# Stick-breaking attention on one core: two heads per ScalarE and VectorE operation, the gate made transposed, the values product turned round

## The chip, the cores and the metric

One core of a Trainium2 chip runs the whole program. The metric is device time in microseconds (us) from launch to end, lower is better. TensorE (PE in the profile, its weight loads PEld) multiplies, ScalarE (ACT) applies functions, VectorE (DVE) does elementwise work, GpSimd (POOL) small side jobs, SyncE (SP) issues most DMAs.

## The reference

Three layers of a small network over 256 tokens of width 1024 are computed one after the other. The change lies in the second, the stick-breaking attention with 16 heads of 64:

```python
def stick_breaking_attention(q, k, v):          # (B, H, S, d)
    for blk in range(S // Q_BLOCK):             # Q_BLOCK = 128, S = 256
        logits = einsum('bhtd,bhsd->bhts', q[:, :, t0:L], k[:, :, :L]) * SB_SCALE
        mask = s_idx < t_idx
        log_keep = where(mask, log_sigmoid(-logits), 0.0)
        later = cumsum(log_keep, reverse=True) - log_keep
        a = where(mask, exp(log_sigmoid(logits) + later), 0.0)
        outs.append(einsum('bhts,bhsd->bhtd', a, v[:, :, :L]))

    # in the block around it
    k_all, v_all = split(rms_norm(x, kv_norm) @ w_kv, 2)
    k_sh, v_sh = rms_norm(heads(k_all), k_norm), heads(v_all)
    q, z = split(rms_norm(x, b_norm) @ b_w_in, 2)
    q = rms_norm(heads(q), b_q_norm)
    o = stick_breaking_attention(q, k_sh, v_sh)
    x = x + (o * silu(z)) @ b_w_out
```

## The kernel before, in words

Each engine runs a program written out by hand, and semaphores tie them together. TensorE multiplies in float32r with both operands split into a high and a low part, so one product of 128x128 by 128x512 is three matmuls (L735, L736, L737). The activations are turned into hT_hi and hT_lo (contraction in the partitions, 256 tokens in the columns); in `product` a piece of hT is stationary and 512 weight columns move.

**Weights.** A block of 1024 x 512 lands in a ring of two and is split in two halves: ScalarE writes whi, then VectorE wlo. The split buffers hold three halves, so the split of a half (`refill(name, half)`, three halves ahead) can begin once TensorE has used the named half. These splits, the copies of results out of PSUM and the head norms stand in a fixed order on ScalarE and VectorE. TensorE's order here is: products k, v, transposes of k ("T k"), product q, product zb (the gate z), with the transposes of q amid it. Each stage has two products of 512 columns (nb = 0, 1). The head norm of half of k or q is `half_means` on VectorE (squares, sum, mean), a power on GpSimd, `half_scale` on VectorE.

**The loop.** 16 heads go in 8 pairs, j = 0 to 7; each head has its bank of PSUM (six banks in turn). For pair j TensorE makes the logits transposed, keys in the partitions, 384 columns a head (`stick_logits`, L885 to L891). ScalarE makes log(1 + exp(-|x|)) of them by Abs (L1465), Exp (L1466), Ln (L1480); VectorE adds max(x, 0) to it (L2085) and splits the sum into sp_hi and sp_lo (L2090, L2094); TensorE then adds the cumulative sums into the same bank (`stick_logs`, L898, L901, L903), ScalarE takes the Exp (L1473, the weights a), and TensorE multiplies by the values (`stick_values`, L912 to L914). LAG is 2, and on TensorE iteration j holds logits(j), logs(j-2), values(j-3); on ScalarE it is Abs and Exp of the first head of j, the two L1473 of j-2, Abs and Exp of the second head, two Ln of j. logits(j) needs the banks of pair j-3, so it waits for both L1473 of j-3. Three `ple` products (L844) stand ahead of logs(0), a fourth after the loop.

**After the loop** the gated result h is turned on TensorE (`turn("o1", ...)`, L728), split by ScalarE (L1303) and VectorE (L1708), and goes into product b_out.

## Time and profile before

| what | value |
|---|---|
| time, median of 3 runs | 868.62 us (868.02 to 869.25) |
| span of the profiled execution, first to last instruction | 866.2 us |
| PE, PEld, DVE, ACT busy | 851.7, 737.0, 591.9, 441.4 us |
| loop, from logits(0) to the fourth ple | 213.13 to 248.33 us |

The profiled execution has only its span; a time of its own outside the span is not given. The span is 2.4 us below the median of the runs, which is what launch and end add. Busy times overlap between engines and, for matmuls, within TensorE: a matmul of 512 columns is listed with some 0.39 us though the next one starts 0.23 us after it. Distances between starts are therefore what counts on TensorE.

### The profile page before, as it was taken

The numbers are of one execution on the slowest core, as the hardware profiler recorded it, in microseconds if no ns is written. First come the engines' busy times: TensorE is split into PE (matmuls) and PEld (weight loads), VectorE is DVE, ScalarE is ACT, GpSimd is POOL, SyncE is SP. The second block draws the span as 40 slices with busy tenths as digits, with TensorE's granted clock in tenths as the row PEclk, the third lists the DMA queues.
The fourth block names the chain that finished last, engine by engine and source line by source line (L and its number), as shares of the span: only waits on it lengthen the run. The fifth ranks groups of instructions, "written<-read, shape, count | busy, mean of one in ns | idle before, by whom it ended". The sixth has DMA issues, their size and how long they took to land.

```text
span 866.2 us, 13480 instructions
## 1 busy us (share of the span) xinstructions
PE 851.7 (98%) x5659; PEld 737.0 (85%) x5659; DVE 591.9 (68%) x738; ACT 441.4 (51%) x591; POOL 117.3 (14%) x74
## 2 busy tenths in 40 slices
PE   8999999999999999999999999999989999999998
PEld 7887888888788887888988889997868999999996
DVE  5684677666756678888788788786975655555553
ACT  6644466556953656754553446443164644444441
POOL 0100001111000004123144344540000000000000
PEclk9999999999999999999999999999999999999999
DMA  9927645555004436226455565556976465555621
GB/s 332 372 75 246 239 146 196 194 194 184 11 22 154 160 98 244 97 97 210 157 198 167 207 231 195 209 190 140 282 265 235 151 210 182 188 190 194 194 98 48
DMA packets 68405, 155.96 MB, mean 180 GB/s; under 512 B 3145, under 2 KB 6954, under 8 KB 68346
## 3 DMA queue, kind: packets, MB, share of 16 engines
q1 hardware_dynamic: 65312, 146.80, 50.1%
q0 software_dynamic: 2224, 7.67, 2.6%
q10 hardware_dynamic: 810, 0.63, 0.5%
q8 instruction: 45, 0.74, 0.3%
q14 instruction: 14, 0.11, 0.0%
HBM read 146.70 MB, written 7.34 MB: 178 GB/s over the span
## 4 chain that ended last, share of the span: by engine, by line
PE 91%; DVE 6%; ACT 2%; issue 1%; DMA 0%; ACTq 0%; DVEq 0%
PE bank L735 19%; PE bank L736 19%; PE bank L737 19%; PE bank L1062 7%; PE bank L1064 7%; PE bank L1060 7%; PE bank L728 3%; PE bank L844 2%; PE bank L834 1%; PE bank L946 1%; PE bank L885 1%; DVE pT L1826 1%; PE bank L1133 1%; PE bank L1122 1%; DMA vrows<-in_vecs 0%
## 5 line engine op out<-in xcount | busy, mean ns | idle before, releaser
L1725 DVE TENSOR_TENSOR wlo<-ring,whi 128x2048 fp32r<-128x2048 f32 (+1 forms) x103 | 251.7, 2449 | 135.3 <-ACT whi L1334 135.0
L1334 ACT ACTIVATE whi<-ring 128x2048 fp32r<-128x2048 f32 (+1 forms) x104 | 198.4, 1909 | 208.3 <-PE bank L737 143.2
L735 PE MATMUL bank<-whi,hT 128*128 128x512 f32 (+1 forms) x512 | 201.6, 394 | 3.2 <-DVE wlo L1955 1.4
L737 PE MATMUL bank<-whi,hT 128*128 128x512 f32 (+1 forms) x512 | 198.8, 388 | 0.0
L736 PE MATMUL bank<-wlo,hT 128*128 128x512 f32 (+1 forms) x512 | 198.7, 388 | 0.0
L1060 PE MATMUL bank<-hT,whi 128*128 128x256 f32 x512 | 145.3, 284 | 0.0
L1062 PE MATMUL bank<-hT,whi 128*128 128x256 f32 x512 | 144.9, 283 | 0.0
L1064 PE MATMUL bank<-hT,wlo 128*128 128x256 f32 x512 | 144.8, 283 | 0.0
L735 PEld LDWEIGHTS bank<-whi,hT 128*128 128x128 f32 x512 | 96.1, 188 | 25.0 <-issue 2.7
L737 PEld LDWEIGHTS bank<-whi,hT 128*128 128x128 f32 x512 | 96.1, 188 | 19.6
L736 PEld LDWEIGHTS bank<-wlo,hT 128*128 128x128 f32 x512 | 96.2, 188 | 19.0 <-issue 0.5
L1060 PEld LDWEIGHTS bank<-hT,whi 128*128 128x128 f32 x512 | 98.2, 192 | 0.6
L1062 PEld LDWEIGHTS bank<-hT,whi 128*128 128x128 f32 x512 | 98.2, 192 | 0.5
L1064 PEld LDWEIGHTS bank<-hT,wlo 128*128 128x128 f32 x512 | 98.2, 192 | 0.0
L735 PE MATMUL bank<-whi,hidT_hi 128*128 128x512 f32 x224 | 88.0, 393 | 0.0
L736 PE MATMUL bank<-wlo,hidT_hi 128*128 128x512 f32 x224 | 87.4, 390 | 0.0
L737 PE MATMUL bank<-whi,hidT_lo 128*128 128x512 f32 x224 | 87.2, 389 | 0.0
L1720 DVE SCALAR_TENSOR_TENSOR wlo<-ring,vcols,whi 128x512 fp32r<-128x512 f32 x64 | 43.8, 745 | 20.6 <-ACT whi L1330 20.6
L1330 ACT ACTIVATE whi<-ring,vcols 128x512 fp32r<-128x512 f32 x64 | 40.9, 711 | 19.3 <-PE bank L737 17.0
L735 PEld LDWEIGHTS bank<-whi,hidT_hi 128*128 128x128 f32 x224 | 42.1, 188 | 9.7 <-issue 1.2
L737 PEld LDWEIGHTS bank<-whi,hidT_lo 128*128 128x128 f32 x224 | 42.1, 188 | 9.0
L736 PEld LDWEIGHTS bank<-wlo,hidT_hi 128*128 128x128 f32 x224 | 42.1, 188 | 8.2
(296 smaller groups left out, 1026.9 us busy)
## 6 DMA issues: line engine op xcount, KB each, us to landing
ring<-in_w_ff SPq DMA_DIRECT2D x64, 1024.0 KB, 5.3
ring<-in_ple_gate_w SPq DMA_DIRECT2D x8, 1024.0 KB, 5.0
ring<-in_w_kv SPq DMA_DIRECT2D x8, 1024.0 KB, 5.0
ring<-in_b_w_in SPq DMA_DIRECT2D x8, 1024.0 KB, 5.0
ring<-in_a_w_in SPq DMA_DIRECT2D x7, 1024.0 KB, 13.1
ring<-in_w_in SPq DMA_DIRECT2D x6, 1024.0 KB, 5.8
ring<-in_w_glu SPq DMA_DIRECT2D x6, 1024.0 KB, 10.1
ring<-in_a_w_out SPq DMA_DIRECT2D x4, 1024.0 KB, 5.7
```

The lines of the kernel that those rows point to most:

```text
L728: last = pe.transpose(b[0:width, cc * S + t * P:cc * S + t * P + P], src[:, t, c * width:(c + 1) * width], ident)
L735: pe.matmul(bank_cols, high[:, at[0], at[1]], w_high, start=first, stop=False)
L736: pe.matmul(bank_cols, high[:, at[0], at[1]], w_low, start=False, stop=False)
L737: return pe.matmul(bank_cols, low[:, at[0], at[1]], w_high, start=False, stop=last)
L844: last = pe.matmul(b[:, :], pT[:, l, k, t * P:(t + 1) * P], ple_rows[:, k, nb * 512:(nb + 1) * 512], start=(k == 0), stop=(k == 1))
L1060: pe.matmul(b[:, at:at + S], w_high[:, kk, cols], hT_hi[:, k, :], start=k == 0 and at == 0, stop=False, skip_group_check=True)
L1062: pe.matmul(b[:, at:at + S], w_high[:, kk, cols], hT_lo[:, k, :], start=False, stop=False, skip_group_check=True)
L1064: last = pe.matmul(b[:, at:at + S], w_low[:, kk, cols], hT_hi[:, k, :], start=False, stop=k == KC - 1, skip_group_check=True)
L1330: ins = act.activation(whi[at][:, n], ring[:, slot[name], cols][:, n], ACT.Copy, scale=gain(gained[name[0]], 4 * (g % 2) + kk))
L1334: act.activation(whi[at], raw_rows(g), ACT.Copy).then_inc(high_made, 1)
L1720: ins = dve.scalar_tensor_tensor(out=wlo[at][:, n], in0=ring[:, slot[name], cols][:, n], scalar=gain(gained[name[0]], 4 * (g % 2) + kk), i ...
L1725: dve.tensor_tensor(wlo[at], raw_rows(g), whi[at], ALU.subtract).then_inc(low_made, 1)
```

## The change

1. **Loop.** The eight banks become one tensor, and `bank_pair` views the two banks of a pair as 2 x 384 columns. Abs, Exp, Exp of the logs, Ln and the three VectorE operations run once per pair on 768 columns. On ScalarE the order is now Abs(j), Exp(j), Exp of the logs(j-2), Ln(j).
2. **Values.** `stick_values` takes a pair: the 64 value columns of a head are stationary, the weights a move (256 and 128 columns). The even head writes partitions 0 to 63, the odd head 64 to 127, so the result is already transposed.
3. **Gate.** z is made transposed by `turned_product`: 128x128 pieces of the weights are stationary and 256 token columns of hT move. Since the norm's scale per token now lies along the columns, `rows_of_rstd` makes a row of it in all partitions: VectorE fills two diagonal tiles (`diag`), TensorE multiplies them by a matrix of -1, VectorE copies the result. VectorE multiplies z by it (`z_out`), and ScalarE takes Silu afterwards from SBUF.
4. **After the loop.** The transposes of o1 are gone; oz = o times gate is split into hT_hi and hT_lo by ScalarE (`oz_split`) and VectorE (`oz_low`), for the most part within the loop's last iterations.
5. **Order.** The products now stand as k, q (with the rows between its two halves), T k, zb (with T q amid it), v, loop; the weight loads likewise.

```diff
-    for stage in ("k", "v"):
-        for nb in range(2):
-            product(stage, nb, (stage, nb), turned_by="kv" if stage == "k" else None, first=(
...
+    def rows_of_rstd():
+        b = begin("rows")
+        pe.wait_ge(diag_ready, NT)
+        for t in range(NT):
+            last = pe.matmul(b[:, t * P:(t + 1) * P], allneg[:, :], diag[:, t, :], start=True, stop=True)
+        last.then_inc(pe_done, 1)
+    def turned_product(name, between=None):
...
+                for c in range(4):
...
+                        pe.matmul(to, w_high[:, kk, cols], hT_hi[:, k, :], start=k == 0 and at == 0, stop=False,
+                        pe.matmul(to, w_high[:, kk, cols], hT_lo[:, k, :], start=False, stop=False,
+                        last = pe.matmul(to, w_low[:, kk, cols], hT_hi[:, k, :], start=False, stop=k == KC - 1,
...
+    for nb in range(2):
+        product("k", nb, ("k", nb), turned_by="kv", first=None if nb else (
+            lambda: turn("kv", x, units=(2, 3), ready=x_gated(0))))
+    product("q", 0, ("q", 0))
+    rows_of_rstd()
+    product("q", 1, ("q", 1))
     turn("k", k_tok, ready=lambda k: pe.wait_ge(heads_normed, 1 + k // 2))
+    turned_product(("zb", 0))
+    turned_product(("zb", 1),
+                   between=lambda: turn("q", q_tok, ready=lambda k: pe.wait_ge(heads_normed, 3 + k // 2)))
     for nb in range(2):
+        product("v", nb, ("v", nb))
...
-        pe.matmul(o[:, 0:HD], a[:, 0:P], vh[:, 0, :], start=True, stop=True)
-        pe.matmul(o[:, HD:P], a[:, P:S], vh[:, 0, :], start=True, stop=False)
-        last = pe.matmul(o[:, HD:P], a[:, S:S + P], vh[:, 1, :], start=False, stop=True)
...
+        for o, vh, a in sides:
+            pe.matmul(o, vh[:, 0, :], a[:, 0:S], start=True, stop=False, skip_group_check=True)
+        for o, vh, a in sides:
+            last = pe.matmul(o[:, P:S], vh[:, 1, :], a[:, S:384], start=False, stop=True, skip_group_check=True)
...
     ple(1, 1, 1)
-    turn("o1", h, ready=lambda k: emptied(("stick_out", k)))
     out_and_gate(1, "b_out", "o1")
...
+        if j < NH // 2:
+            filled(("logits", 2 * j + 1))
+            if j >= 2:
+                act.wait_ge(sp_ready, j - 1)
+            act.activation(logs[:, two, :], bank_pair("logits", j), ACT.Abs).then_inc(abs_ready, 1)
+            act.wait_ge(abs_ready, j + 1)
+            act.activation(logs[:, two, :], logs[:, two, :], ACT.Exp, scale=-1.0).then_inc(exps_ready, 1)
+        if j >= LAG:
+            c = j - LAG
+            filled(("loga", 2 * c + 1))
+            act.activation(sticks[:, 2 * (c % 2):2 * (c % 2) + 2, :], bank_pair("loga", c), ACT.Exp)\
+                .then_inc(act_emptied, 2)
+        if j < NH // 2:
+            act.wait_ge(exps_ready, j + 1)
+            act.activation(logs[:, two, :], logs[:, two, :], ACT.Ln, bias=1.0).then_inc(logs_ready, 1)
+        else:
+            oz_split(j - NH // 2)
...
     half_means(k_tok, 1)
-    refill(("v", 0), 0)
+    refill(("q", 0), 0)
     half_scale(k_tok, 1)
...
+    dve.wait_ge(rstd_ready, 2)
+    for t in range(NT):
+        dve.tensor_scalar(diag[:, t, :], ident, rstd[:, 1, t:t + 1], None, ALU.mult).then_inc(diag_ready, 1)
+    refill(("q", 0), 1)
+    b = filled("rows")
+    dve.tensor_copy(neg_rows, b[:, 0:S]).then_inc(dve_emptied, 1)
```

**VectorE around the norm of k.** Before, the program of VectorE reads, from the squares of the second half of k on (L2034 to L2036 are `half_means`, L1720 the split of a half, L2042 `half_scale`):

```order
L2034 TENSOR_TENSOR aux<-work 128x1024 [waits act_emptied]
L2035 TENSOR_REDUCE ssh<-aux 128x16 [waits dve_step]
L2036 TENSOR_SCALAR msh<-ssh 128x16 [waits dve_step]
L1720 SCALAR_TENSOR_TENSOR wlo<-ring,vcols,whi 128x512 [waits high_made]
L1720 SCALAR_TENSOR_TENSOR wlo<-ring,vcols,whi 128x512 x3
L2042 TENSOR_TENSOR work<-work,rsh 128x2x512 [waits headr_ready]
L1720 SCALAR_TENSOR_TENSOR wlo<-ring,vcols,whi 128x512 [waits high_made]
```

Of the change the same place reads (L2106 to L2108 are now `half_means`, L2114 `half_scale`, L2129 the diagonals, L2132 the copy of the row):

```order
L2106 TENSOR_TENSOR aux<-work 128x1024 [waits act_emptied]
L2107 TENSOR_REDUCE ssh<-aux 128x16 [waits dve_step]
L2108 TENSOR_SCALAR msh<-ssh 128x16 [waits dve_step]
L1792 SCALAR_TENSOR_TENSOR wlo<-ring,vcols,whi 128x512 [waits high_made]
L1792 SCALAR_TENSOR_TENSOR wlo<-ring,vcols,whi 128x512 x3
L2114 TENSOR_TENSOR work<-work,rsh 128x2x512 [waits headr_ready]
L2129 TENSOR_SCALAR sig<-cst,rstd 128x128 [waits rstd_ready]
L2129 TENSOR_SCALAR sig<-cst,rstd 128x128
L1792 SCALAR_TENSOR_TENSOR wlo<-ring,vcols,whi 128x512 [waits high_made]
L1792 SCALAR_TENSOR_TENSOR wlo<-ring,vcols,whi 128x512 x3
L2132 COPY sig<-bank 128x256 [waits pe_done]
```

The two diagonals have come in behind `half_scale`, which waits for GpSimd's power (headr_ready).

**TensorE between the two products of q, in the change** (L751 to L753 are the three matmuls of `product`, L890 the rows):

```order
L753 MATMUL bank<-whi,hT 128x512
L890 MATMUL bank<-sig,allneg 128x128 [waits diag_ready,dve_emptied]
L890 MATMUL bank<-sig,allneg 128x128
L751 MATMUL bank<-whi,hT 128x512 [waits low_made,act_emptied,dve_emptied]
L752 MATMUL bank<-wlo,hT 128x512
```

Before, a product followed the other here with no matmul between; now every later matmul stands behind the wait on diag_ready.

**ScalarE in one iteration of the loop.** Before:

```order
L1465 ACTIVATE aux<-bank 128x384 [waits sp_ready,pe_done]
L1466 ACTIVATE aux<-aux 128x384 [waits act_step]
L1473 ACTIVATE aux<-bank 128x384 [waits pe_done] x2
L1465 ACTIVATE aux<-bank 128x384 [waits sp_ready,pe_done]
L1466 ACTIVATE aux<-aux 128x384 [waits act_step]
L1480 ACTIVATE aux<-aux 128x384 [waits exps_ready] x2
```

Of the change, from the Ln of the iteration before to the Abs of the next one:

```order
L1549 ACTIVATE aux<-aux 128x768 [waits exps_ready]
L1539 ACTIVATE aux<-bank 128x768 [waits sp_ready,pe_done]
L1541 ACTIVATE aux<-aux 128x768 [waits abs_ready]
L1545 ACTIVATE aux<-bank 128x768 [waits pe_done]
L1549 ACTIVATE aux<-aux 128x768 [waits exps_ready]
L1539 ACTIVATE aux<-bank 128x768 [waits sp_ready,pe_done]
```

Eight instructions have become four, and the Exp of the logs (L1545), whose end frees the banks for the next logits, now stands behind an Abs and an Exp of both heads.

## Rows read from the trace of the kernel before

**Rows 1.** Page, part 1 and part 2: busy time, granted clock by slices.
```profile
PE 851.7 (98%) x5659; PEld 737.0 (85%) x5659; DVE 591.9 (68%) x738; ACT 441.4 (51%) x591; POOL 117.3 (14%) x74
...
PEclk9999999999999999999999999999999999999999
```

**Rows 2.** Page, part 4: the chain that ended last.
```profile
PE 91%; DVE 6%; ACT 2%; issue 1%; DMA 0%; ACTq 0%; DVEq 0%
```

**Rows 3.** Waits of PE, the longest: us, times, longest.
```profile
PE bank L1214 <- DVE aux L1836: 1.9, 2, 1.8
```

**Rows 4.** Timeline around k's head norm: start us, us, engine, line, what, idle before.
```profile
155.30 0.69 ACT L1281 ACTIVATE work<-bank,rstd 128x512 f32<-128x512 f32 x1 [2.03 <-PE bank L737]
...
153.01 3.33 POOL L2387 TENSOR_TENSOR rsh<-msh,half_neg 128x16 f32<-128x16 f32 x1 [7.54 <-DVE msh L2036]
...
156.38 1.23 DVE L2042 TENSOR_TENSOR work<-work,rsh 128x1024 f32<-128x1024 f32 x1 [0.81 <-POOL rsh L2387]
```

**Rows 5.** Timeline of PE, products of 512 columns (70 records).
```profile
189.74 0.39 PE L736 MATMUL bank<-wlo,hT 128*128 128x512 f32 x1
...
205.38 0.39 PE L736 MATMUL bank<-wlo,hT 128*128 128x512 f32 x1
```

**Rows 6.** Timeline of PE, products of 256 columns elsewhere (37 records).
```profile
413.81 0.28 PE L1062 MATMUL bank<-hT,whi 128*128 128x256 f32 x1
...
418.12 0.28 PE L1062 MATMUL bank<-hT,whi 128*128 128x256 f32 x1
```

**Rows 7.** Timeline of PE, the loop's start, one iteration, and its end.
```profile
213.13 0.70 PE L885 MATMUL bank<-work 64*128 64x256 f32 x4
...
223.73 0.70 PE L885 MATMUL bank<-work 64*128 64x256 f32 x4 [0.63 <-ACT aux L1473]
...
234.74 0.70 PE L885 MATMUL bank<-work 64*128 64x256 f32 x4
235.27 0.39 PE L887 MATMUL bank<-work 64*128 64x128 f32 x4
235.59 0.23 PE L890 MATMUL bank<-bf 128*128 128x128 bf16 x1
...
235.83 0.44 PE L898 MATMUL bank<-aux,allneg 128*128 128x128 f32 x2
...
237.04 0.33 PE L912 MATMUL bank<-work,aux 128*128 128x64 f32 x2
...
238.41 0.70 PE L885 MATMUL bank<-work 64*128 64x256 f32 x4
...
248.33 1.94 PE L844 MATMUL bank<-ple_rows,pT 128*128 128x512 f32 x4
250.11 1.91 PE L728 MATMUL bank<-cst,h 128*128 128x128 f32 x16
252.32 0.47 PE L735 MATMUL bank<-whi,hT 128*128 128x512 f32 x1 [0.31 <-DVE hT L1708]
```

**Rows 8.** Timeline of ACT in the loop: the first L1473, then one iteration.
```profile
222.57 1.06 ACT L1473 ACTIVATE aux<-bank 128x384 f32<-128x384 f32 x2 [0.90 <-PE bank L903]
...
235.91 0.49 ACT L1465 ACTIVATE aux<-bank 128x384 f32<-128x384 f32 x1
236.44 0.52 ACT L1466 ACTIVATE aux<-aux 128x384 f32<-128x384 f32 x1
236.87 0.85 ACT L1473 ACTIVATE aux<-bank 128x384 f32<-128x384 f32 x2
```

**Rows 9.** Timeline of ACT, a larger operation elsewhere.
```profile
125.88 1.06 ACT L1348 ACTIVATE h<-x 128x1024 f32<-128x1024 f32 x1
```

**Rows 10.** Timeline of DVE, last pair.
```profile
242.78 1.02 DVE L2085 SCALAR_TENSOR_TENSOR aux<-bank,aux 128x384 f32<-128x384 f32 x2 [0.58 <-ACT aux L1480]
...
244.25 1.02 DVE L2094 TENSOR_TENSOR sp_lo<-aux,sp_hi 128x384 fp32r<-128x384 f32 x2
```

**Rows 11.** Timeline of PE, stationary operands of 32 columns in four column groups.
```profile
615.72 1.52 PE L1200 MATMUL bank<-spare,work 128*32 128x128 f32 x48
```

More of the change, by code:

```diff
@@ L191, in plan @@
     gemm(u, "k", 2, "a")
-    gemm(u, "v", 2, "a")
+    for t in range(NT):
+        u.add(("q", 0, t), "a")
+    u.add("rows", "v")
+    for t in range(NT):
+        u.add(("q", 1, t), "a")
     turned(u, "k")
-    gemm(u, "q", 2, "a")
-    gemm(u, ("zb", 0), 1, "a")
+    gemm(u, ("zb", 0), 1, "v")
     for k in range(4):
         u.add(("T", "q", k), "va"[k % 2], bank=2 + k)
-    u.add((("zb", 1), 0, 0), "a", bank=6)
-    u.add((("zb", 1), 0, 1), "a", bank=7)
+    for n in range(2):
+        u.add((("zb", 1), 0, n), "v", bank=6 + n)
+    for nb in range(2):
+        for t in range(NT):
+            u.add(("v", nb, t), "a", bank=2 + 4 * nb + t)
     for j in range(NH // 2 + LAG + 1):
@@ L338, in loads @@
     two("k", w_kv, 0, "k")
-    two("v", w_kv, D, "v")
     two("q", b_in, 0, "q")
@@ L403, in sem @@
             return ctx.enter_context(nc.semaphore(name))
-        ps = [ctx.enter_context(nc.psum_tensor(f"bank{i}", [P, 512], F32)) for i in range(8)]
+        bank_all = ctx.enter_context(nc.psum_tensor("bank", [P, 8 * 512], F32))
+        ps = [bank_all[:, 512 * i:512 * i + 512] for i in range(8)]
         x = sb("x", [P, NT, D])
@@ new lines, in turned_product @@
+            def turned_product(name, between=None):
+                banks = [begin((name, 0, n)) for n in range(2)]
+                for half in range(2):
+                    g = 2 * order[name] + half
+                    w_high, w_low = part_views(g, 4, 512)
+                    pe.wait_ge(low_made, g + 1)
+                    for c in range(4):
+                        cols = slice(c * P, (c + 1) * P)
+                        at = S * (c % 2)
+                        to = banks[c // 2][:, at:at + S]
+                        for kk in range(4):
+                            k = 4 * half + kk
+                            pe.matmul(to, w_high[:, kk, cols], hT_hi[:, k, :], start=k == 0 and at == 0, stop=False,
+                                      skip_group_check=True)
+                            pe.matmul(to, w_high[:, kk, cols], hT_lo[:, k, :], start=False, stop=False,
+                                      skip_group_check=True)
+                            last = pe.matmul(to, w_low[:, kk, cols], hT_hi[:, k, :], start=False, stop=k == KC - 1,
+                                             skip_group_check=True)
+                        if half and c % 2:
+                            last.then_inc(pe_done, 1)
+                        elif half == 0 and c == 3:
+                            last.then_inc(first_used, 1)
+                    if between and half == 0:
+                        between()
@@ L872, in _ @@
             for nb in range(2):
-                product("q", nb, ("q", nb), turned_by=None)
-            product(("zb", 0), 0, ("zb", 0))
-            product(("zb", 1), 0, ("zb", 1),
-                    between=lambda: turn("q", q_tok, ready=lambda k: pe.wait_ge(heads_normed, 3 + k // 2)))
+                product("v", nb, ("v", nb))
             pe.wait_ge(masks_ready, 5)
@@ L1440, in _, with silu_of_z @@
             for nb in range(2):
+                refill(("q", nb), 0)
+                tokens_out("q", nb, q_tok, 1)
+                refill(("q", nb), 1)
+            turned_out("k", [(kT, "k_norm", True)])
+            def silu_of_z(n):
+                act.wait_ge(dve_emptied, u.emptied((("zb", n // 2), 0, n % 2)))
+                zv = zT[:, 2 * n:2 * n + 2, :]
+                act.activation(zv, zv, ACT.Silu).then_inc(z_ready, 1)
+            refill(("zb", 0), 0)
+            silu_of_z(0)
+            silu_of_z(1)
+            refill(("zb", 0), 1)
+            refill(("zb", 1), 0)
+            turned_out("q", [(qT, "q_norm", True)])
+            refill(("zb", 1), 1)
+            silu_of_z(2)
+            silu_of_z(3)
+            act.preload_act_table_set("natural_log_exp_and_others")
+            for nb in range(2):
                 refill(("v", nb), 0)
@@ L1444, in _ @@
                     refill(("v", 0), 1)
-            refill(("v", 1), 1)
-            turned_out("k", [(kT, "k_norm", True)])
-            for nb in range(2):
-                refill(("q", nb), 0)
-                tokens_out("q", nb, q_tok, 1)
-                refill(("q", nb), 1)
-            for nb in range(2):
-                refill(("zb", nb), 0)
-                for t in range(NT):
-                    copy_out((("zb", nb), 0, t), z_tok[:, t, 512 * nb:512 * nb + 512], None, rstd[:, 1, t:t + 1], ACT.Silu)
-                if nb == 0:
-                    refill(("zb", 0), 1)
-                    turned_out("q", [(qT, "q_norm", True)])
@@ L1481, in _, with oz_split @@
-            copy_out(("ple1", 1, 1), pl_tok[1][:, 1, 512:D])
-            turned_high("o1", None)
-            refill(("zb", 1), 1)
+            def oz_split(m):
+                act.wait_ge(dve_emptied, u.emptied(("stick_out", m)))
+                act.activation(hT_hi[:, 2 * m:2 * m + 2, :], oz[:, 2 * m:2 * m + 2, :], ACT.Copy).then_inc(oz_high, 1)
+            for j in range(NH // 2 + LAG):
+                two = slice(2 * (j % 2), 2 * (j % 2) + 2)
+                if j < NH // 2:
[15 more added lines that the diff above has]
+                    oz_split(j - NH // 2)
```

140 lines of the change are left out of this document (75 added, 65 removed).

## The prediction

> **What bounds the kernel now.** I read the page's busy line first: TensorE is busy 98% of the span and its clock stands at its upper level, 2.4 GHz, in every slice [rows 1]. Since matmul durations overlap, the chain that ended last is the better witness: 91% of it is TensorE [rows 2]. TensorE's longest wait for anybody is 1.8 us [rows 3]. So a change here pays only by what it does to the distances between TensorE's starts, and a wait put into its queue is lost one for one, unless work in front of it was waited for anyway.
>
> The loop shows the same. From 234.74 to 238.41 one iteration takes 3.67 us without a gap [rows 7]: logits 1.09 (234.74 to 235.83), logs 1.21 (to 237.04), values 1.37 (to 238.41). Beside it ScalarE starts Abs 1.17 us after the logits, Exp 0.53 later, the two L1473 0.43 after that, for 0.85 us [rows 8]. They end at 237.72. The logits that need them could follow 0.10 us later, by the one place where they had to wait (ScalarE's pair ends at 223.63, TensorE starts at 223.73) [rows 7, 8]. They start only at 238.41: TensorE sets the pace, with 0.6 us in hand.
>
> **1. The rows of rstd: a new stall.** In the changed order the first q product stands where the first v product stood; the result copy at 155.30 [rows 4] shows that this product's last start-to-start slot ends at about 155.10 (the copy starts as a record ends, and a record outlives its slot of 0.23 us by 0.16). TensorE's next instruction is now the rows, which wait for two diagonal tiles. VectorE writes these behind `half_scale` of the second half of k, which waits for GpSimd's power. Nothing ahead of it moves: the power runs from 153.01 to 156.34, `half_scale` from 156.38 to 157.61 [rows 4]. Two small VectorE operations follow; no row has their size, so I take 0.2 us each, between 0 and the 0.5 of a 384-column one [rows 10], and the matmul starts at 158.05. TensorE stands for **2.95 us** (2.6 to 3.5), and behind it in its queue are the second q product and all that follows. No cover exists; ScalarE's and VectorE's splits merely get more slack. The two matmuls themselves: four records, at a quarter of the 0.445 us that a record of 512 columns takes in the fourth ple (1.78 us from 248.33 to 250.11 for four) [rows 7], are **0.43 us**, plus 0.09 for changing between kinds of matmul (the first record of b_out lasts 0.47 in place of 0.39) [rows 5, 7].
>
> **2. The gate transposed.** 96 matmuls of 512 columns become 192 of 256. The first go at (205.38 - 189.74)/69 = 0.2267 us each [rows 5], the second at (418.12 - 413.81)/36 = 0.1197 us [rows 6]. 192 x 0.1197 - 96 x 0.2267 = **+1.24 us**. The Silu operations keep their count. The four multiplications by the row are new on VectorE, and the split of later weights queues behind them; VectorE is idle a third of the span and I take the split to be in time, at most 1 us late. Moving the v products behind z costs TensorE nothing, and SyncE's queue gets the same loads in another order. It has a use: a table load and the last Silu no longer stand between the loop's start and its first Abs. But logs(0) stands behind three ple in any case, so this is worth nothing.
>
> **3. The loop.** The values of a pair fall from 1.37 to about 0.85 us: two row halves take 0.53 us for 256 columns and 0.32 for 128 [rows 7], and column groups run side by side as well (48 records of 128 columns take 1.52 us, 0.03 each, where one in a row of them takes 0.11) [rows 11]. In turn they could cost 1.28. So TensorE would need 3.15 us an iteration. But the cycle through ScalarE grows. logits(j+1) needs the Exp of the logs(j-2), and before this ScalarE has now Abs and Exp of both heads of j. The sizes: Exp from SBUF takes 0.52 us for 384 columns [rows 8] and 1024 columns take 1.06 [rows 9], so 384 more cost 0.32. The cycle is
>  - logits until Abs of both heads: 1.17 + 0.12 for the second head's mask matmuls = 1.29
>  - Abs to the dependent Exp: 0.53 + 0.32 = 0.85
>  - Exp to the next, independent one: 0.43 + 0.32 = 0.75
>  - Exp of the logs, to its end: 0.80 (Abs of 384 from the same bank is 0.49 [rows 8], and 0.32 on top)
>  - its end to the next logits: 0.10
>
> in all **3.79 us**, more than 3.67 and far more than 3.15. ScalarE's own work fell (it now idles in each iteration while the logits run); what grew is the ping-pong. logits(3) start at 224.07 instead of 223.73 (both heads' logs end 0.6 us after the first, 222.57 + 0.60 + 0.80 + 0.10) [rows 7, 8], 10.94 after the loop's start, and four cycles bring logits(7) to +26.1 us from the loop's start instead of +25.28 (238.41 - 213.13). So at its last logits the loop has lost 0.8 us.
>
> The Trainium skill, "Perfetto Trace Analysis", section "Optimizing Scalar/DVE Operations", has both sides: larger operations help if the engine is saturated; where it is not but causes bubbles, breaking instructions up may get work done sooner. By the rows ScalarE has idle time while it waits for logits, so the second half applies; by the first half, the loop would run at 3.15 us.
>
> **4. The end of the loop.** Before, from logits(7) to the first b_out matmul: 252.32 - 238.41 = 13.91 us [rows 7]. After: Abs at 1.29, Exp 2.14, Exp of logs(5) 2.89, Ln 3.64 to 4.48, VectorE's three operations 2.5 (242.78 to 245.27 for the same columns) [rows 10] to 7.0; then 0.6 for the rest of logs(7) and 0.4 until ScalarE starts, 8.0; Exp 0.80, wait 0.10, values 0.85, 9.75; ple 1.78, and b_out follows at 11.5. The 2.21 us from 250.11 to 252.32 for the transposes and their wait are gone, since oz 0 and 1 are split during the loop, and oz 2 and 3 have b_out's first half (24 x 0.2267 = 5.4 us) as cover. Gain 2.4, with the 0.8 lost: **-1.6 us** for loop and end.
>
> **The sum.** 2.95 + 0.43 + 0.09 + 1.24 - 1.6 = **+3.1 us**. The span goes from 866.2 to 869.3. The median lies 2.4 us above the span before; with the same 2.4 the time is **871.7 us**, 0.36% slower.
>
> **Bounds.** Stall 2.6 to 3.5. VectorE late with a split: 0 to 1. ScalarE's 768-column operations between 0.05 us less each (loop -2.4 in all) and twice those of 384 (cycle 1.29 + 1.02 + 0.86 + 0.96 + 0.10 = 4.23: 1.8 us more in four cycles and 0.6 at the end, so +0.8). Values side by side or in turn matter only for the last pair: 0.43. Likely together: 870.4 to 873.4; all the dear ends at once would be 875.8.
>
> **Rivals.**
> - *Loop at TensorE's pace* (not slower). The place is the Exp of the logs. If it is not behind both others in effect, logits(7) are at 10.9 + 4 x 3.15 = 23.5, the end 11.5 later, 35.0 against 39.19: -4.2 in place of -1.6, total +0.5, **869.1**. This decides once the cycle through ScalarE is under 3.15 us, 0.64 below my sum; nothing in the rows for 384 and 1024 columns allows that. 0.14.
> - *The clock falls in the stall.* No gap of the trace is longer than 1.8 us, and the clock stays up in all; the new one is 2.95. If half the 5.4 us of matmuls behind it ran at 1.2 GHz, that costs 2.7 more: **874.4**. 0.12. The Trainium skill, "TensorE: Matmul & The Clock Gate", section "Why this matters for your kernels", warns that idle gaps between bursts of matmuls can put the clock back to the lower level; no gap here shows it.
> - *The stall is not there*, because the diagonals come early or TensorE gets past them: +0.15, **868.8**, no change. Against it stands the order of instructions alone, strongly. 0.08.
> - *Faster* for a reason that I don't see, or two of the above together: 0.06, about 866.
>
> **Chances.** Mine has 0.60, at 871.7, 870.4 to 873.4. Some 0.2% (1.7 us) is what a measurement of this kernel can tell from no change. Slower: 0.58 of mine and the clock's 0.12, 0.70. No change: the loop's rival, most of the missing stall and a little of mine, 0.22. Faster: 0.08. For 8 in 10 the range is 869.0 to 874.4.
>
> **What would show it.** In the changed kernel's trace: one PE wait of about 2.9 us just after 155 us, on VectorE's diagonals, with the granted clock 1.00 beside it; matmuls of 256 columns 0.12 apart; the loop's start at about 217.8; iterations of 3.8 us with some 0.6 us idle on TensorE ahead of each logits, ended by ScalarE's Exp; b_out right behind the fourth ple. Wrong would be: a period near 3.2, no wait at the rows, a wait for wlo in the products, or a lower clock.

## The result and the profile after

The changed kernel takes 874.16 us in the median of 4 runs (873.24 to 876.60), the kernel before 868.38 in 4 (868.02 to 869.25): a ratio of 1.0073, 95% interval 1.0059 to 1.0086. It is 5.8 us slower, where 3.1 had been forecast. The profiled execution of after took 873.58 us with a span of 871.8, 5.6 more than the span before. Time and span of one execution are 1.8 us apart, here and in every run on record; the 2.4 us named ahead for launch and end compared the median of before with the span of a faster execution.

The page of the changed kernel answers to [rows 1, 2]:

```profile
PE 851.3 (98%) x5711; PEld 735.1 (84%) x5711; DVE 594.3 (68%) x717; ACT 438.5 (50%) x559; POOL 116.6 (13%) x74
...
PEclk9999999999999999999999999999999999999999
...
PE 88%; DVE 7%; ACT 3%; issue 1%; DMA 0%; POOL 0%; ACTq 0%; DVEq 0%
```

TensorE's waits (us in total, times, longest) answer to [rows 3]:

```profile
PE bank L939 <- ACT aux L1545: 3.1, 5, 1.0
PE bank L890 <- DVE sig L2129: 2.9, 1, 2.9
```

TensorE has 88% of the chain, where it had 91%; DVE has 7% and not 6. Two new waits head the list, one for the loop's exponential, one for the diagonals. The clock's line by slices shows nothing, since a slice is 22 us long.

Timeline of VectorE around the diagonals (start, us, engine, line, what, idle before), answering to [rows 4], and behind it that of TensorE:

```profile
156.31 1.23 DVE L2114 TENSOR_TENSOR work<-work,rsh 128x1024 f32<-128x1024 f32 x1 [0.81 <-POOL rsh L2482]
157.45 0.48 DVE L2129 TENSOR_SCALAR sig<-cst,rstd 128x128 f32<-128x128 f32 x2
```

```profile
154.81 0.39 PE L753 MATMUL bank<-whi,hT 128*128 128x512 f32 x1
158.08 0.68 PE L890 MATMUL bank<-sig,allneg 128*128 128x128 f32 x4 [2.88 <-DVE sig L2129]
158.51 0.48 PE L751 MATMUL bank<-whi,hT 128*128 128x512 f32 x1
158.83 0.39 PE L752 MATMUL bank<-wlo,hT 128*128 128x512 f32 x1
159.06 0.56 PE L753 MATMUL bank<-whi,hT 128*128 128x512 f32 x1
159.42 0.63 PE L751 MATMUL bank<-whi,hT 128*128 128x512 f32 x1
...
162.41 0.46 PE L752 MATMUL bank<-wlo,hT 128*128 128x512 f32 x1
162.71 0.40 PE L753 MATMUL bank<-whi,hT 128*128 128x512 f32 x1
```

Without the rows the next product matmul would start 0.23 us behind 154.81; it starts at 158.51, 3.47 us late, and the step to the one behind it is 0.32 in place of 0.23, the change of kind that the prediction had at 0.09. Then something else happens: from 159.06 the starts are 0.36 to 0.43 us apart instead of 0.227, with 0.30 as the last such step, and from 162.71 on 0.23 again. Nine steps take 3.65 us instead of 2.04. The same stretch by windows (busy us of PE, PEld, DVE, ACT, POOL, then the granted clock) says why:

```profile
155.00:158.00 3.00, 0.19 (x1) 0.00 (x0) 2.12 (x4) 2.77 (x5) 1.28 (x1) 1.00 0.37 100
158.00:159.50 1.50, 1.42 (x8) 1.27 (x9) 1.10 (x2) 0.36 (x1) 0.00 (x0) 0.88 1.06 411
159.50:162.00 2.50, 2.50 (x8) 1.92 (x7) 2.50 (x5) 0.00 (x0) 0.00 (x0) 0.50 0.16 60
163.00:168.00 5.00, 5.00 (x24) 4.12 (x23) 1.03 (x2) 2.05 (x4) 2.90 (x1) 1.00 0.50 191
```

The granted clock is 0.50, the level of 1.2 GHz, over 2.5 us in which TensorE is busy all the time: it fell about 1 us after TensorE had resumed work, and came back some 3.5 us later.

One iteration of the loop on TensorE, and the next on ScalarE, answering to [rows 7, 8]:

```profile
234.28 0.70 PE L939 MATMUL bank<-work 64*128 64x256 f32 x4 [0.52 <-ACT aux L1545]
...
238.06 0.70 PE L939 MATMUL bank<-work 64*128 64x256 f32 x4 [0.52 <-ACT aux L1545]
```

```profile
239.35 0.81 ACT L1539 ACTIVATE aux<-bank 128x768 f32<-128x768 f32 x1 [0.66 <-PE bank L945]
240.19 0.85 ACT L1541 ACTIVATE aux<-aux 128x768 f32<-128x768 f32 x1
240.94 0.80 ACT L1545 ACTIVATE aux<-bank 128x768 f32<-128x768 f32 x1
241.63 0.83 ACT L1549 ACTIVATE aux<-aux 128x768 f32<-128x768 f32 x1
```

238.06 - 234.28 = 3.78 us is the period. TensorE idles 0.52 us ahead of the logits, for ScalarE's Exp of the logs, and ScalarE 0.66 us for the logits: each waits for the other.

The loop's end on TensorE, where b_out begins:

```profile
255.44 1.98 PE L862 MATMUL bank<-ple_rows,pT 128*128 128x512 f32 x4
256.86 0.80 PE L751 MATMUL bank<-whi,hT 128*128 128x512 f32 x1
257.49 0.40 PE L752 MATMUL bank<-wlo,hT 128*128 128x512 f32 x1
```

The first b_out record starts 0.03 us behind the last of the four ple records (256.83), though these stand 0.43 us apart. Its start therefore says little of when its work begins, and the account goes by the second, at 257.49; before, the second started at 252.63.

**The accounts, at places of TensorE's timeline**, after minus before:

| term | forecast | measured |
|---|---|---|
| rows: stall, their matmuls, the change of kind | 2.95 + 0.43 + 0.09 = 3.47 | 3.04 + 0.43 + 0.09 = 3.56 |
| clock behind the stall | 0 | 3.65 - 2.04 = 1.61 |
| gate: what is left of the loop's later start (219.53 against 213.13) | 1.24 | 6.40 - 3.56 - 1.61 = 1.23 |
| loop's first logits to b_out's second matmul (37.96 against 39.50) | -1.6 | -1.54 |
| from b_out's second matmul until the stage at 606 us | 0 | 0.6 |
| from there to the end | 0 | 0.1 |

That is 5.6, the span's difference. The 3.04 of the stall run from 155.04, where the slot of the last product matmul ends, to 158.08; the profile's 2.88 count from the end of that matmul's record.

### The profile page after: what moved, and what is told of

Its sections match the earlier page's. It is cut to its first block, busy times and chain, and to the rows that moved or that the text cites. A ratio compares the mean times of both kernels' runs of the same rounds, so it can differ in the third digit from the quotient of the medians.

```text
span 871.8 us, 13529 instructions
## 1 busy us (share of the span) xinstructions
PE 851.3 (98%) x5711; PEld 735.1 (84%) x5711; DVE 594.3 (68%) x717; ACT 438.5 (50%) x559; POOL 116.6 (13%) x74
## 4 chain that ended last, share of the span: by engine, by line
PE 88%; DVE 7%; ACT 3%; issue 1%; DMA 0%; POOL 0%; ACTq 0%; DVEq 0%
PE bank L751 18%; PE bank L753 17%; PE bank L752 17%; PE bank L1121 7%; PE bank L1123 7%; PE bank L1119 7%; PE bank L744 3%; PE bank L862 2%; PE bank L908 1%; PE bank L906 1%; PE bank L910 1%; PE bank L852 1%; ACT aux L1545 1%; DVE wlo L1792 1%; PE bank L939 1%
## 5 line engine op out<-in xcount | busy, mean ns | idle before, releaser
L751 PE MATMUL bank<-whi,hT 128*128 128x512 f32 (+1 forms) x480 | 190.4, 397 | 2.9 <-DVE wlo L2027 1.5
L753 PE MATMUL bank<-whi,hT 128*128 128x512 f32 (+1 forms) x480 | 187.3, 390 | 0.0
L752 PE MATMUL bank<-wlo,hT 128*128 128x512 f32 (+1 forms) x480 | 187.1, 390 | 0.0
L751 PEld LDWEIGHTS bank<-whi,hT 128*128 128x128 f32 x480 | 90.6, 189 | 23.5 <-DVE wlo L2027 2.5
L753 PEld LDWEIGHTS bank<-whi,hT 128*128 128x128 f32 x480 | 90.5, 189 | 18.6
L752 PEld LDWEIGHTS bank<-wlo,hT 128*128 128x128 f32 x480 | 90.7, 189 | 18.1 <-issue 0.7
L751 PE MATMUL bank<-whi,hidT_hi 128*128 128x512 f32 x224 | 88.1, 393 | 0.0
L753 PE MATMUL bank<-whi,hidT_lo 128*128 128x512 f32 x224 | 87.3, 390 | 0.0
L751 PEld LDWEIGHTS bank<-whi,hidT_hi 128*128 128x128 f32 x224 | 42.1, 188 | 9.6 <-issue 1.2
L753 PEld LDWEIGHTS bank<-whi,hidT_lo 128*128 128x128 f32 x224 | 42.1, 188 | 8.9
```

What stands on the lines that cost most here:

```text
L751: pe.matmul(bank_cols, high[:, at[0], at[1]], w_high, start=first, stop=False)
L752: pe.matmul(bank_cols, high[:, at[0], at[1]], w_low, start=False, stop=False)
L753: return pe.matmul(bank_cols, low[:, at[0], at[1]], w_high, start=False, stop=last)
```

## The experiments

All were run with the kernel before beside them on the same chip; medians and ranges are given with the ratio to it. In the diffs a minus is the changed kernel's line, unless said otherwise.

**1. The changed kernel again.** No edit.

> The changed kernel once more, as the base of the others. Both theories: 874 us, with one PE wait of 2.9 us at the rows and some 3.4 us of lower clock behind it. If the clock stays at 1.000 in a run, the theory that the clock costs 1.6 us expects that run near 872.6.

873.55 us (873.14 to 874.29, 5 runs), before 868.49 (17 runs), ratio 1.0055 (1.0043 to 1.0067). The stall of 2.88 us and the steps at 0.43 us are there again, two records later (nine steps from 159.51 to 163.16, 3.65 us), and the loop takes the same 37.33 us to b_out's first record. It is the reference for what follows: what the change costs repeats. The test in its expectation failed: one of the five executions had its clock at 1.000 and took 873.89 us, not some 872.6, and the one at 1.000 of the four executions of the result (873.24) was hardly faster than the others. Neither was profiled. So the 1.6 us of the clock are shown on TensorE's timeline, in executions that were profiled, and not in the times; whether the read-out stage of experiment 2 took them there isn't known.

**2. The diagonals early.** They are written behind the first half of `half_scale` on k, while TensorE is still in the product.

```diff
             half_scale(k_tok, 0)
+            dve.wait_ge(rstd_ready, 2)
+            for t in range(NT):
+                dve.tensor_scalar(diag[:, t, :], ident, rstd[:, 1, t:t + 1], None, ALU.mult).then_inc(diag_ready, 1)
...
             half_scale(k_tok, 1)
-            dve.wait_ge(rstd_ready, 2)
-            for t in range(NT):
-                dve.tensor_scalar(diag[:, t, :], ident, rstd[:, 1, t:t + 1], None, ALU.mult).then_inc(diag_ready, 1)
```

> The two diagonals are written behind the first half_scale of k, where VectorE idled. Theory (the wait of 2.95 us on the rows and the lower clock behind it, 1.6 us, are the larger part of the loss): 869.6 us, no wait at the rows, clock 1.000. Rival (the wait only uncovers another one behind it, or the rest of the change carries the loss): above 872 us.

Timeline of TensorE at the same place:

```profile
155.07 0.40 PE L753 MATMUL bank<-whi,hT 128*128 128x512 f32 x1
155.30 0.61 PE L890 MATMUL bank<-sig,allneg 128*128 128x128 f32 x4
155.67 0.48 PE L751 MATMUL bank<-whi,hT 128*128 128x512 f32 x1
```

No wait, no slow records. b_out starts at 252.38, in the changed kernel at 256.86: 4.48 us are gone, the stall with the 1.6 of the clock. Yet the median falls by 2.7 only, to 870.82 (868.23 to 873.25, 11 runs), ratio 1.0023 (1.0010 to 1.0035), between the 869.6 of the theory and the 872 of the rival. Its profiled execution gives 3.3 us back in one stage, the read-out of the state layer, at 606 to 641 us; the last part of this section is about that.

**3. The stall kept, TensorE kept busy in it.** 13 matmuls of no use go into the rows' bank, which the rows then overwrite.

```diff
                 b = begin("rows")
+                for _ in range(13):
+                    pe.matmul(b[:, 0:P], allneg[:, :], allneg[:, :], start=True, stop=True, skip_group_check=True)
                 pe.wait_ge(diag_ready, NT)
```

> The diagonals stay late, but 13 extra matmuls of 128 columns, whose result is overwritten, run on TensorE in the 2.9 us gap. Theory (idle time there lowers the clock, and that costs 1.6 us by itself): 872.6 us, granted clock 1.000, the rows still start at about 158. Rival (the lower clock has another cause): 874 us and clock 0.998.

TensorE's timeline, and the window behind it:

```profile
155.37 0.40 PE L753 MATMUL bank<-whi,hT 128*128 128x512 f32 x1
155.60 3.07 PE L889 MATMUL bank<-allneg 128*128 128x128 f32 x26
158.55 0.71 PE L892 MATMUL bank<-sig,allneg 128*128 128x128 f32 x4
159.01 0.47 PE L751 MATMUL bank<-whi,hT 128*128 128x512 f32 x1
```

```profile
158.20:162.80 4.60, 4.60 (x26) 3.87 (x25) 4.12 (x8) 0.74 (x2) 0.00 (x0) 1.00 0.51 194
```

TensorE is late by the same time, but never idle, and the clock is 1.00. From the last product matmul ahead of the rows to the loop's first logits it is 63.06 us (155.37 to 218.43), 64.74 in experiment 1 (154.79 to 219.53), 59.97 in experiment 2 (155.07 to 215.04). So the stall itself is 3.1 and the clock 1.7: **two prices of one wait**, and the second is for idleness, not for lateness. The median, 874.48 (872.75 to 878.00, 6 runs), ratio 1.0072 (1.0053 to 1.0090), doesn't show it: taken alone it is what the rival expected, 874 us, and so is the whole execution's clock of 0.997. The trace puts both in another place: the clock fell at 631.7 us, in the read-out stage, and that stage took back 1.4 us of the 1.7.

**4. Half of it kept busy.** The same with `range(6)`.

> The changed kernel with 6 instead of 13 matmuls of no use ahead of the wait for the diagonals: they cover about 1.4 of the 2.9 us, so TensorE stands idle for about 1.5 us. It asks how long a gap it takes here. If it is the length of the gap that brings the clock down, no record at half speed follows: the product behind the rows steps at 0.23 us throughout and b_out starts 1.6 us earlier than in the changed kernel, at 255.3. If any gap at this place does it, records of 0.63 us at 0.43 us follow, and b_out starts at 256.9.

```profile
155.40 1.50 PE L889 MATMUL bank<-allneg 128*128 128x128 f32 x12
158.35 0.71 PE L892 MATMUL bank<-sig,allneg 128*128 128x128 f32 x4 [1.44 <-DVE sig L2131]
...
161.66 0.39 PE L751 MATMUL bank<-whi,hT 128*128 128x512 f32 x1
161.89 0.39 PE L752 MATMUL bank<-wlo,hT 128*128 128x512 f32 x1
```

Behind a gap of 1.44 us no record is slow; b_out starts at 255.55, 1.3 us ahead of experiment 1 although this execution was 0.4 late at 155. It is a single execution, 872.29 us, with the clock at 1.000. As far as one can show it, it matters at this place how long the gap is.

**5. Logs before logits.** On top of experiment 2, TensorE writes logs(j-2) ahead of logits(j), and ScalarE takes their Exp first.

```diff
-                if j < NH // 2:
+                if j < NH // 2 and j <= LAG:
                     stick_logits(j)
...
                         stick_logs(i)
+                if LAG < j < NH // 2:
+                    stick_logits(j)
```

> Diagonals early as in the run before the last, and in the loop logs(j-2) come ahead of logits(j) on TensorE and the Exp of the logs ahead of Abs and Exp on ScalarE, from j = 3 on. Theory (the loop's period of 3.77 us is a ping-pong: logits, Abs, Exp, Exp of the logs, logits): the period falls to TensorE's own 3.15 us, the loop gets 3 us shorter and the time is 866.5 us. Rival (operations on two banks or larger operations are themselves what is slow): period stays above 3.6 us, time 869 us or more.

873.62 us (873.11 to 874.20, 5 runs), ratio 1.0056 (1.0044 to 1.0068): the remedy made it worse. From the loop's start to b_out it takes 41.06 us, and 37.34 in experiment 2. TensorE:

```profile
232.18 0.70 PE L939 MATMUL bank<-work 64*128 64x256 f32 x4
...
236.10 0.45 PE L957 MATMUL bank<-sp_lo,tneg_r 128*128 128x384 f32 x1 [0.55 <-DVE sp_lo L2193]
...
237.05 0.70 PE L939 MATMUL bank<-work 64*128 64x256 f32 x4
```

The logits now stand behind the logs, and these wait for VectorE's three operations on the pair two iterations back, which came too late (0.55 us at 236.10): a ping-pong over VectorE took the place of that over ScalarE, and logits alternate 3.3 and 4.9 us apart. By its numbers this is the outcome that the rival expected; experiments 6 and 7 decide between the two.

**6. Single heads again.** On top of experiment 2, ScalarE and VectorE take one head at a time in the order of before. ScalarE's part of it:

```diff
-                    act.activation(logs[:, two, :], bank_pair("logits", j), ACT.Abs).then_inc(abs_ready, 1)
-                    act.wait_ge(abs_ready, j + 1)
-                    act.activation(logs[:, two, :], logs[:, two, :], ACT.Exp, scale=-1.0).then_inc(exps_ready, 1)
...
+                if j < NH // 2:
+                    stick_exp(2 * j)
+                for i in (2 * (j - LAG), 2 * (j - LAG) + 1):
+                    if i >= 0:
+                        b = filled(("loga", i))
+                        act.activation(sticks[:, i % 4, :], b[:, 0:384], ACT.Exp).then_inc(act_emptied, 1)
+                if j < NH // 2:
+                    stick_exp(2 * j + 1)
```

> The kernel with the diagonals early, and in the stick-breaking loop ScalarE and VectorE work on one head at a time again, in the order of the kernel before; the transposed gate and the values with stationary v stay. Theory (the period of 3.77 us is a ping-pong: the weights' exponential of pair j-2 stands behind the absolute value and the exponential of both heads of pair j, 1.29 + 0.85 + 0.75 + 0.80 us behind the logits): with single heads the exponential of the logs waits only for one head's two operations, so the period falls to about 3.45 us, b_out starts 1.3 to 2 us ahead of the kernel with the diagonals early, and the time is 869.3 at most where the read-out stage takes nothing back. Rival (the period is set by the work of ScalarE, so that fewer and wider operations are what helps): eight operations of one head in place of four of two cost 8 x about 0.2 us a pair more, the period goes to 3.9 or above, and b_out comes 1 us later or more.

**7. One place earlier.** Two heads an operation, but ScalarE takes the Exp of the logs between Abs and Exp of the new pair.

```diff
                     act.activation(logs[:, two, :], bank_pair("logits", j), ACT.Abs).then_inc(abs_ready, 1)
-                    act.wait_ge(abs_ready, j + 1)
-                    act.activation(logs[:, two, :], logs[:, two, :], ACT.Exp, scale=-1.0).then_inc(exps_ready, 1)
                 if j >= LAG:
                     c = j - LAG
                     filled(("loga", 2 * c + 1))
                     act.activation(sticks[:, 2 * (c % 2):2 * (c % 2) + 2, :], bank_pair("loga", c), ACT.Exp)\
                         .then_inc(act_emptied, 2)
+                if j < NH // 2:
+                    act.wait_ge(abs_ready, j + 1)
+                    act.activation(logs[:, two, :], logs[:, two, :], ACT.Exp, scale=-1.0).then_inc(exps_ready, 1)
```

> The kernel with the diagonals early, and ScalarE's order in the loop changed by one place: absolute value of pair j, exponential of the logs of pair j-2, exponential of pair j, logarithm of pair j. All stays at two heads an operation, and TensorE's order is that of the changed kernel. Theory (ping-pong): the next logits wait for the exponential of the logs, which now comes right behind the absolute value: 1.29 + 0.8 to 1.2 + 0.8 + 0.1 = 3.0 to 3.4 us, so ScalarE's four operations (0.81 + 0.85 + 0.80 + 0.83 = 3.29 plus their gaps of 0.1) set a period of 3.3 to 3.5 us, no wait of TensorE for logits above 0.3 us, b_out 1.8 to 2.5 us ahead of the kernel with the diagonals early, time 868.0 to 869.5. Rival (the loop is bound by ScalarE's load or by the chain over VectorE, as the order with the logs first ran into): the period stays at 3.7 or above and b_out moves by less than 0.5 us.

Logits in experiment 6, then in experiment 7:

```profile
232.75 0.70 PE L939 MATMUL bank<-work 64*128 64x256 f32 x4 [0.20 <-ACT aux L1546]
236.20 0.70 PE L939 MATMUL bank<-work 64*128 64x256 f32 x4 [0.20 <-ACT aux L1546]
```

```profile
233.59 0.70 PE L939 MATMUL bank<-work 64*128 64x256 f32 x4 [0.21 <-ACT aux L1543]
...
237.06 0.70 PE L939 MATMUL bank<-work 64*128 64x256 f32 x4 [0.21 <-ACT aux L1543]
```

The periods are 3.45 and 3.47 us where the expectations had 3.45, and 3.3 to 3.5: the ping-pong was the cause of 3.78, and either more and smaller operations or another order breaks it. In 7 ScalarE's four operations still have the sizes of the changed kernel, so their load was not the bound. Loop start to b_out is 35.04 us in experiment 6, better by 2.3 than two heads at a time. In experiment 7 it is 36.63, only 0.7 better: the last logits come 1.3 earlier, but the end takes 11.80 us in place of 11.25. The last pair's Ln is the fourth operation in either order, but now starts 4.13 us behind its logits, not 3.58, mainly because ScalarE reaches the Exp of logs(5) before TensorE has them ready, and waits 0.35 us. Against the expectation b_out didn't move there, also because that execution was 0.6 us late before the loop. Times: 868.63 us (866.17 to 871.42, 11 runs), ratio 1.0005 (0.9995 to 1.0015), and 869.60 (868.00 to 872.33, 11 runs), ratio 1.0011 (1.0002 to 1.0020).

**8. The banks of before in the new kernel, and the reverse.** Ahead of o2's transposes the change takes seven banks fewer in turn (o1's four are gone, v's four are fixed ones now, the rows add one). In a round of eight that is one place further: the transposes stand in banks 6, 7, 0, 1, not 5, 6, 7, 0, and the second meets the bank of soft_out 3, not of soft_out 2. Experiment 8a is experiment 2 with the round set back; 8b is the kernel before with `u.turn += 1` instead.

```diff
+    u.turn -= 1
     turned_in_two(u, "o2")
```

> The kernel with the diagonals early, and the turn of the banks set back by one ahead of the transposes of o2, so that they and what follows stand in the banks of the kernel before. Theory: the wait of 0.6 us of o2's second transpose for the bank of soft_out 3 goes, -0.3 us from there. Of the stage of 606 to 641 us, where the kernel with the diagonals early lost 3.3 us in one execution: if the turned banks cause it, the median falls to 868.5 to 869 and the scatter to that of the kernel before (868.0 to 870.4); if it has another cause, the median is 870.5 and the times still reach over 872.5.

> The kernel before with one edit: the turn of the banks set on by one ahead of the transposes of o2, so that they stand in the banks of the changed kernel. Theory: +0.3 us at o2's second transpose, as in the changed kernel, and 868.8 in all if that is everything. If the turned banks are also what makes the stage at 606 to 641 us lose up to 3 us in some executions, the median is 869.5 or more and some times are over 871.

TensorE at o2's transposes before, in 8a, then in 8b:

```profile
384.63 2.27 PE L728 MATMUL bank<-cst,h 128*128 128x128 f32 x16
```

```profile
385.22 2.28 PE L745 MATMUL bank<-cst,h 128*128 128x128 f32 x16
```

```profile
384.40 0.61 PE L729 MATMUL bank<-cst,h 128*128 128x128 f32 x4
385.59 1.53 PE L729 MATMUL bank<-cst,h 128*128 128x128 f32 x12 [0.58 <-DVE h L2219]
```

The wait comes and goes with the bank, and so does its price: from o2's first transpose to the first product matmul behind it are 2.17 or 2.18 us in the profiles of before and of experiments 8a, 9 and 10, and 2.47 in all others, 8b among them. That is 0.30 us. 8b has 868.76 us (868.10 to 869.74, 11 runs), ratio 1.0005 (0.9997 to 1.0014). 8a has 870.04 us (868.19 to 873.98, 12 runs), ratio 1.0025 (1.0012 to 1.0039): no fall of the scatter, so the turned banks are not its cause.

**9. All three.** Diagonals early, single heads, banks set back; run twice.

> Three edits of the changed kernel together: the diagonals early, single heads on ScalarE and VectorE in the loop, and the turn of the banks set back by one ahead of o2. Theory: b_out starts at 250.3 us as with single heads (2.0 us ahead of before), o2's wait adds nothing, so TensorE reaches the read-out stage at 606 us 1.6 to 2.0 us ahead of the kernel before; without losses there the time is 866.2 to 866.8, and the median is 867 to 868.3, since the read-out stage has taken up to 3 us in some executions of every kernel with this gate and loop so far. Rival: what is won ahead of 606 us is always given back there, since that stage is paced by its transfers; then the median is 868.4 or more, like the kernel before.

> The kernel with all three edits once more, since its first interval, 0.9981 to 1.0001, only just holds no change. If it is truly 0.7 us ahead of the kernel before, the ratio is again between 0.998 and 1.000 and the lowest times lie 2 us below those of the kernel before; if the first median was luck, the ratio comes out over 1.0.

867.57 us (865.69 to 869.92, 12 runs), ratio 0.9991 (0.9981 to 1.0001), and 866.74 (865.58 to 872.56, 12 runs), ratio 0.9983 (0.9967 to 0.9999). The lowest times lie 2.0 and 2.2 us below those of before, as the second expectation had it. This version is 6 to 7 us faster than the changed kernel. It is probably faster than the kernel before as well, by 0.1 to 0.2% in the median; its scatter is larger, and two of its 24 executions (872.40 and 872.56) are slower than all but one of the 40 of before beside them.

**10. More matmuls of no use in the read-out stage.** Experiment 9 with `KEEP = (0, 3, 12, 9)` for `(0, 3, 12, 5)`.

> The same, with nine in place of five matmuls of no use ahead of the second half's read-out, where TensorE waits for transfers. Theory (the scatter comes from idle time of over 2 us in the read-out stage, behind which the clock falls, as behind the 2.9 us stall at 155 us): with four more matmuls at 0.23 to 0.28 us each the idle time there is 1 us shorter, clocks below 0.999 become rare, the highest times fall from 871 to about 869, at a price of 0 to 0.3 us in the lowest. Rival (the scatter is the transfers' own, the clock only a part of it): highest times over 870.5 remain, and the median is that of the kernel without the four.

868.40 us (866.32 to 871.68, 12 runs), ratio 1.0003 (0.9991 to 1.0015). The high times remained (871.68 and 870.92), as the rival had it; whether the median is that of experiment 9 or somewhat above it, these runs don't tell.

**What the read-out stage takes.** From the first transposes of that stage (tile xg_at) to the first product behind it, in the profiled executions:

| kernel | us |
|---|---|
| before; after; experiments 1, 4, 5, 8a, 8b, 9 first | 31.1 to 31.2 |
| 3, 6 | 32.6 |
| 2, 7 | 34.4, 34.5 |
| 10; 9 second | 36.5, 37.3 |

It isn't the code alone: experiment 9's two profiles are of one kernel, and have 31.1 and 37.3. TensorE in the second, with two windows behind it:

```profile
612.22 5.90 PE L1239 MATMUL bank<-work 128*64 128x32 f32 x112 [1.36 <-issue]
...
636.65 0.64 PE L1274 MATMUL bank<-ring,aux 64*32 64x128 f32 x5 [2.93 <-issue]
637.94 3.65 PE L1287 MATMUL bank<-cst,work 128*128 128x128 f32 x16 [0.65 <-ACT work L1706]
```

```profile
612.00:618.00 6.00, 5.78 (x112) 5.77 (x112) 5.90 (x7) 0.00 (x0) 0.00 (x0) 0.55 0.76 220
636.60:642.50 5.90, 5.20 (x24) 4.32 (x25) 1.75 (x4) 3.75 (x7) 0.00 (x0) 0.50 0.73 259
```

and in the first, where the same two groups take 3.46 and 1.94 us:

```profile
610.51 3.46 PE L1239 MATMUL bank<-work 128*64 128x32 f32 x112 [0.28 <-issue]
...
631.99 1.94 PE L1287 MATMUL bank<-cst,work 128*128 128x128 f32 x16 [1.00 <-DVE work L2444]
```

Both gaps are followed by half the clock (0.55 and 0.50), as at 155 us. So the loss has the form of the first one: a wait, and then the clock.

The profile names no releaser of these waits ("issue"), but the traces narrow down what they are. The profiled executions with the new gate have 24 unnamed waits of 0.25 us or more of TensorE between 590 and 645 us, and 23 of them stand at one of four places: ahead of the 3823rd, 3949th, 4204th or 4331st matmul record of the program. It is a place in the count, not in the work. Experiment 3 has 26 records more ahead of it and waits 2.13 us at the 4204th, which there is one of L1261, and in experiment 10, with four more in the read-out, the last wait comes after 119 records of one read-out line where it comes after 123 in experiments 2, 7 and 9. And all 23 end 1.3 to 1.6 us after a packet of 16 KB on the DMA queue that the profile calls "q8 instruction": in experiment 9's second profile such packets run from 609.57 to 610.80 and from 634.11 to 635.12, and TensorE goes on at 612.22 and 636.65. So what TensorE waits for there is its own instructions, by all that the traces show. No experiment was made for it, and why the packets come late in one execution and not in the other is open: that of 634.11 started 0.39 us after TensorE had stopped. It fits that the added matmuls of experiment 10 were no remedy: in its profile TensorE ran the first of the nine and then waited 0.60 us, at the 4204th record, before the others.

## Why the prediction was wrong, and where it was right

**The rows' stall** was forecast to 0.1 us: 3.04 for 2.95, counted as there from the end of the last slot, the whole step 3.56 for 3.47. It rests on one reading, that in the new order the rows stand where GpSimd's power is still ahead of VectorE's queue. Experiment 2 shows it by taking it away.

**The step that failed** is "with the granted clock 1.00 beside it". The fall of the clock was a rival at 0.12 and no part of the sum, on the ground that "no gap of the trace is longer than 1.8 us, and the clock stays up in all". That row said nothing of a gap of 2.9; it should have made the rival as likely as not. It costs 1.6 us by the steps behind the stall, 1.7 by experiments 1 against 3, and my price for it, 2.7, was too high: I had half the clock for 5.4 us, and it was there for some 3.5. In experiment 4's one execution a gap half as long was free of it. The rule named there, of the Trainium skill, "TensorE: Matmul & The Clock Gate", section "Why this matters for your kernels", that gaps between bursts can put the clock back, agrees with the trace: 0.50 behind the gap of 2.88 us.

**The gate** cost what was forecast, 1.23 for 1.24. **The loop** too: logits(3) 10.98 us behind the loop's start (forecast 10.94), logits(7) 26.08 (26.1), the cycle 3.78 (3.79), the end 11.25 to b_out's first record and 11.88 to its second (11.5), with 0.52 us idle ahead of the logits (0.6). The mechanism stands by experiments 6 and 7, whose periods it gave beforehand. "Loop at TensorE's pace" was wrong. Of the two sides of the rule in "Perfetto Trace Analysis", section "Optimizing Scalar/DVE Operations", of the Trainium skill, the second held: with idle time on ScalarE, broken-up operations made the loop 2.3 us shorter.

**A term left out.** The banks: 0.30 us at o2, by experiments 8a and 8b. I had followed what the change moves near itself, but not the round of the banks, whose shift by one place came to bear 130 us later. That is half of the 0.6 us that are lost from b_out to the stage at 606 us. The rest is no more than executions of one kernel differ by: from the product behind o2 to that stage are 218.46 us before, 218.66 in the profile of after, and 218.44 in experiment 1. With 1.6 of the clock and less than 0.1 each for rows, loop and the last stretch, these are the 2.4 us between the forecast and the spans' difference. Some sums of the prediction are off in the last place: the rows' four quarters of 0.445 are 0.445, not 0.43, the gate's difference comes to 1.22 or 1.23, not 1.24, and all dear ends at once to 876.1, not 875.8. None of them matters here. Measured in time, the median of 874.16 is just inside the range up to 874.4; against the kernel before, which ran 0.2 us lower this time, the ratio of 1.0073 is above the 1.0067 that its end stands for.

**Still open** is what decides how late the instructions come in the read-out stage. It took nothing in the two profiles of the changed kernel, so the 5.6 us don't hang on it, but it hides up to 6 us of what is won earlier, and makes medians a poor measure of a change of 1 or 2 us. The places of TensorE's timeline ahead of it were the better measure.

## What to carry to other kernels

A new wait on the engine that bounds a kernel has two prices, its length and what the clock does behind it. If no row shows a gap as long as the new one, take the fall as one of the likely cases; here it was nine instructions at up to twice their distance. Two heads in one operation save fixed time, but where two engines hand work to and fro, each hand-over gets the length of the larger operation; write down the cycle operation by operation, and look at the order in it first. And where buffers are taken in turn, list the whole program's turns before and after, since removing one shifts all that follow. If a wait without a releaser stands at the same count of instructions in kernels with different edits, look at the DMA queue of the instructions before looking at the work around it.

## What was not expected of the hardware

At 155 us the clock fell about 1 us after TensorE had resumed work, not in the gap: the first two product matmuls behind it still stepped at 0.32 and 0.23 us, and the window up to 159.5 has 0.88. It isn't always so. In experiment 3 and in the second profile of experiment 9 it fell within the wait, as these windows with TensorE idle show:

```profile
631.70:631.95 0.25, 0.00 (x1) 0.00 (x0) 0.25 (x1) 0.16 (x1) 0.00 (x0) 0.50 0.88 360
636.50:636.65 0.15, 0.00 (x1) 0.00 (x1) 0.00 (x0) 0.00 (x0) 0.00 (x0) 0.50 0.21 82
```

All six waits of 2.1 us and more in the profiles have a fall of the clock in them or behind them. Of the shorter ones some have and some haven't: a gap of 1.44 us left the clock up at 155 us (experiment 4), one of 1.79 did before at 629 us, and one of 1.36 in the read-out stage was followed by 0.55 over 6 us (second profile of experiment 9). So the length of one gap alone is not what decides, and no run here isolates what else does.

A wait for instructions, if the reading of the read-out stage is right, held TensorE for up to 2.93 us, in a stage of many short matmuls.
